# A two-block transformer on one core: the row factor of five RMS norms applied to the outputs of the linears that follow

## The reference, cut to what matters

```
def rmsnorm(x, g):
    y = xf * lax.rsqrt(jnp.mean(xf * xf, axis=-1, keepdims=True) + RMS_EPS)
    return (y * g).astype(x.dtype)

def hybrid_layer(...):
    h = rmsnorm(x, norm_mix)
    proj = h @ w_in                     # q_a, k_a, v_a, f_a, q_b, kv_b, g_b, gate_a, gate_b
    ...                                 # fox attention, compression, nsa attention with partial_rope
    mixed = jax.nn.sigmoid(gate_a) * y_a + jax.nn.sigmoid(gate_b) * y_b
    x = x + mixed @ w_out
    h = rmsnorm(x, norm_mlp)
    return x + jnp.square(jax.nn.relu(h @ w_up)) @ w_down
```

## Time and profile before

| | |
|---|---|
| median of three runs | 2520.76 us (2517.28 to 2521.58) |
| the profiled execution's own time | 2515.49 us |
| its span | 2513.7 us, 30926 instructions |
| PE busy | 2370.2 us, 94% of the span |
| DVE, POOL, ACT busy | 1485.4, 1512.8, 604.9 us |
| mean granted clock of PE, as a share of full speed | 0.972 |

### The profile page before, as it was taken

How to read it: one execution, slowest core, us unless ns; L and a number is a source line. 1 busy time by engine, 2 the same in 40 slices (tenths; PEclk the granted TensorE clock), 3 DMA queues, 4 the chain that set the end, 5 groups by cost and what they waited for, 6 DMA issues and landing times.

```text
span 2513.7 us, 30926 instructions
## 1 busy us (share of the span) xinstructions
PE 2370.2 (94%) x11516; PEld 1930.5 (77%) x11516; DVE 1485.4 (59%) x1955; ACT 604.9 (24%) x1305; POOL 1512.8 (60%) x677
## 2 busy tenths in 40 slices
PE   4987999999998999999999999989899999999998
PEld 4675778888876778888778888768688877788886
DVE  6798546675142156998485084340569985770742
ACT  3214612221012134342121021121253431210210
POOL 3670058888865641335778788655513348697884
PEclk9998989999999999999999999999999999999999
DMA  4220023223322310111323333223201113233322
GB/s 168 76 84 9 1 67 101 93 100 100 101 85 83 118 59 18 51 43 59 92 76 101 97 96 100 85 78 107 76 10 51 43 53 96 71 104 97 97 96 75
DMA packets 53694, 195.87 MB, mean 78 GB/s; under 512 B 5952, under 2 KB 5952, under 8 KB 53312
## 3 DMA queue, kind: packets, MB, share of 16 engines
q1 hardware_dynamic: 51408, 187.72, 23.6%
q10 hardware_dynamic: 2160, 6.37, 0.7%
HBM read 191.97 MB, written 2.10 MB: 77 GB/s over the span
## 4 chain that ended last, share of the span: by engine, by line
PE 68%; DVE 25%; issue 3%; ACT 1%; POOL 1%; DMA 0%; DVEq 0%; SPq 0%; POOLq 0%; ACTq 0%
PE bank L386 19%; PE bank L387 19%; PE bank L388 19%; DVE sg L1103 4%; PE bank L478 3%; DVE sg L1101 3%; PE bank L509 3%; DVE cols L1115 2%; DVE cols L1129 2%; DVE conv_acc L1044 2%; PE bank L489 1%; DVE on L1134 1%; DVE tmp L1396 1%; DVE cmp_g L1303 1%; PE bank L451 1%
## 5 line engine op out<-in xcount | busy, mean ns | idle before, releaser
L336 POOL TENSOR_TENSOR w_hi<-w_raw,zero 128x1024 fp32r<-128x1024 f32 x336 | 659.6, 1963 | 948.9 <-PE bank L388 923.5
L339 POOL TENSOR_TENSOR w_lo<-w_raw,w_hi 128x1024 fp32r<-128x1024 f32 x336 | 855.7, 2547 | 26.4
L386 PE MATMUL bank<-hn_hi,w_hi 128*128 128x512 f32 x1632 | 667.1, 409 | 20.8 <-DVE hn_lo L1027 14.3
L388 PE MATMUL bank<-hn_hi,w_lo 128*128 128x512 f32 x1632 | 643.0, 394 | 0.0
L387 PE MATMUL bank<-hn_lo,w_hi 128*128 128x512 f32 x1632 | 642.8, 394 | 0.0
L386 PEld LDWEIGHTS bank<-hn_hi,w_hi 128*128 128x128 f32 x1632 | 311.6, 191 | 91.7 <-issue 23.3
L388 PEld LDWEIGHTS bank<-hn_hi,w_lo 128*128 128x128 f32 x1632 | 310.5, 190 | 67.3
L387 PEld LDWEIGHTS bank<-hn_lo,w_hi 128*128 128x128 f32 x1632 | 311.5, 191 | 64.1 <-issue 4.9
L1152 DVE TENSOR_TENSOR x<-bank,x 128x512 f32<-128x512 f32 x64 | 44.3, 692 | 467.3 <-PE bank L388 467.3
L386 PE MATMUL bank<-hid_hi,w_hi 128*128 128x512 f32 x688 | 267.6, 389 | 0.0
L387 PE MATMUL bank<-hid_lo,w_hi 128*128 128x512 f32 x688 | 267.6, 389 | 0.0
(11 more groups left out here) (270 smaller groups left out, 3140.4 us busy)
## 6 DMA issues: line engine op xcount, KB each, us to landing
w_raw<-wstream SPq DMA_DIRECT2D x352, 512.0 KB, 3.6
x<-xT SPq DMA_DIRECT2D x4, 512.0 KB, 9.7
out<-yout ACTq DMA_DIRECT2D x8, 256.0 KB, 2.2
mem_x<-memT SPq DMA_DIRECT2D x1, 1024.0 KB, 15.9
lnc<-lncount ACTq DMA_DIRECT2D x1, 1024.0 KB, 4.8
cs<-trig ACTq DMA_DIRECT2D x2, 512.0 KB, 3.4
par<-params ACTq DMA_DIRECT2D x1, 707.5 KB, 6.4
fc<-fconst ACTq DMA_DIRECT2D x1, 592.0 KB, 8.7
```

Of the source, the lines that this page charges most:

```text
L336: nc.gpsimd.tensor_tensor(w_hi[:, slot, :], w_raw[:, slot, :], zeros, ALU.add).then_inc(w_rounded, 1)
L339: nc.gpsimd.tensor_tensor(w_lo[:, slot, :], w_raw[:, slot, :], w_hi[:, slot, :].bitcast(f32), ALU.subtract).then_inc(w_split, 1)
L386: nc.tensor.matmul(ps[bank][:, 0:cols_], wh, a_h, start=c == 0, stop=False)
L388: mm = nc.tensor.matmul(ps[bank][:, 0:cols_], wl, a_h, start=False, stop=c == chunks - 1)
```

## The change

**Norms 2 to 6.** ACT writes `hn_hi = x*g` straight from the residual, chunk by chunk as tiles are added (`norm_ahead`), and VectorE writes `hn_lo = x*g - hn_hi` inside `add_residual`. The row factor is kept in an SBUF tile `rs` (128 x 512) and multiplied into linears' outputs: by a VectorE multiplication in PSUM (`scale`), or within the instruction that takes the output out. PE starts the next pair of tiles on unscaled activations and has `norm_mean` after its chunk 3 and `norm_spread` behind it.

**Layers' inputs.** `HEAD2` is reordered (and the weight stream with it): the forget gate first, compression inputs third and fifth. VectorE multiplies the rotary table `cs2` by `rs` once a layer; the rotation reads the unscaled PSUM bank. VectorE's queue is in order, and its rotation of job i stands behind its `scale` of job i + 2.

**Gates.** VectorE takes gate tiles out (times `rs`), ACT applies Tanh of half the value in place, and `mix` uses 1 + tanh and a factor 0.5: no reciprocal is left.

**Feed-forward.** UP1 is pipelined by one step; in the layers relu and factor are one VectorE instruction, and ACT makes both the square (into `sq`) and its rounded copy.

```diff
-        HEAD2 = [("cmp", 0), ("cmp", 1), ("gate", 0)] + [("kz", i) for i in range(4)]
+        HEAD2 = [("gate", 0), ("kz", 0), ("cmp", 0), ("kz", 1), ("cmp", 1), ("kz", 2), ("kz", 3)]
...
-            def linear_pair(ta, tb, ready):
+            def linear_pair(ta, tb, ready, n=None):
                 for c in range(DC):
                     linear(ta, hn_hi, hn_lo, S, DC, ready, part=(c, c + 1))
                     linear(tb, hn_hi, hn_lo, S, DC, part=(c, c + 1))
+                    if n is not None and c == 3:
+                        norm_mean(n)
+                if n is not None:
+                    norm_spread(n)
...
-                        if kind == "gate":
-                            pe.wait_ge(*took(t))
-                            turn_tile(fgs[:, :], 4, TT, 32).then_inc(fg_turned, 1)
-                    if 0 <= i - 2 < len(jobs) and tiles[jobs[i - 2]][0] == "gate":
+                    if i == 2:
+                        pe.wait_ge(*took(jobs[0]))
+                        turn_tile(fgs[:, :], 4, TT, 32).then_inc(fg_turned, 1)
+                    if i == 4:
                         pe.wait_ge(fg_log, l + 1)
...
+            def norm_ahead(n, ts_):
+                for c in range(DC):
+                    act.wait_ge(dve_took, tiles[ts_[c]][6])
+                    A(hn_hi[:, c, :], x[:, c, :], ACT.Identity, scale=pcol(NORM_G[n], c)).then_inc(norm_hi, 1)
...
+                    A(sq[:, c % 2, :], x[:, c, :], ACT.Square).then_inc(norm_sq, 1)
+                act.wait_ge(norm_sum, n + 1)
+                A(rt[:, 0:TT], ps[7][:, 0:TT], ACT.Sqrt, bias=pcol("eps")).then_inc(norm_rt, 1)
+                act.wait_ge(norm_row, n + 1)
+                A(rs[:, :], ps[7][:, :], ACT.Copy).then_inc(rs_kept, 1)
...
-                        A(sg[:, g, :], ps[3][:, :], ACT.Exp, scale=-1.0).then_inc(act_took, 1)
+                        act.wait_ge(*took(gate_tiles[g]))
+                        A(sg[:, g, :], sg[:, g, :], ACT.Tanh, scale=0.5).then_inc(gated, 1)
...
+            def scale(t):
+                dve.wait_ge(blocks_done, filled(t))
+                bank = ps[tiles[t][4]]
+                V.tensor_tensor(bank[:, :], bank[:, :], rs[:, :], ALU.mult).then_inc(rs_applied, 1)
...
-                            link(V.tensor_scalar(sg[:, g, :], sg[:, g, :], 1.0, None, ALU.add))
-                        part = slice(quarter * P, (quarter + 1) * P)
-                        link(V.reciprocal(sg[:, g, part], sg[:, g, part]))
+                        dve.wait_ge(blocks_done, filled(gate_tiles[g]))
+                        V.tensor_tensor(sg[:, g, :], ps[3][:, :], rs[:, :], ALU.mult).then_inc(dve_took, 1)
...
                     V.tensor_tensor(x[:, m, :], ps[tiles[t][4]][:, :], x[:, m, :], ALU.add).then_inc(dve_took, 1)
-                    if n is not None and m >= 2:
+                    if n is not None and 2 <= m < DC - 1:
+                        norm_add(n, m - 1)
+                    if n is not None and n < 7:
+                        dve.wait_ge(norm_hi, DC * n + m + 1)
+                        V.scalar_tensor_tensor(out=hn_lo[:, m, :], in0=x[:, m, :], scalar=pcol(NORM_G[n], m),
+                                               in1=hn_hi[:, m, :].bitcast(f32), op0=ALU.mult,
+                                               op1=ALU.subtract).then_inc(norm_lo, 1)
+                    if n is not None and m == DC - 1:
                         norm_add(n, m - 1)
...
-                    if m == 1:
-                        link(V.tensor_scalar(sg[:, 15, :], sg[:, 15, :], 1.0, None, ALU.add))
-                        link(V.reciprocal(sg[:, 15, :], sg[:, 15, :]))
```

More of the change, by code:

```diff
@@ L258, in build, with idx_of_rope @@
             LIN.append(ph)
+        def idx_of_rope(t):
+            return tiles[t][1] + (4 if tiles[t][0] == "kr" else 0)
         def filled(t):
@@ L269, in build @@
         NORM_AFTER = {2: OUT1, 3: DN1, 4: LIN[0]["out"], 5: LIN[0]["down1"], 6: LIN[1]["out"], 7: LIN[1]["down1"]}
+        SCALED = {}
+        for t in UP1 + [t for ph in LIN for t in ph["in"] if tiles[t][0] in ("gate", "kz", "cmp", "v")]:
+            SCALED[t] = len(SCALED) + 1
         NORM_G = {0: "mix_g", 1: "mem_g", 2: "ffn_g", 3: "norm_mix0", 4: "norm_mlp0", 5: "norm_mix1",
@@ L651, in _ @@
                 linear(t, mix_hi, mix_lo, S, DC)
[L652 to L653 removed]
+            linear_pair(UP1[0], UP1[1], (norm_lo, 2 * DC), 2)
             for t in UP1[2:]:
@@ L918, in _ @@
                 ph = LIN[l]
-                norm(3 + 2 * l, x, hn_hi)
-                act.wait_ge(blocks_done, B_L + l * LAYER_BLOCKS)
+                norm_ahead(3 + 2 * l, LIN[0]["down1"] if l else DN1)
                 act.dma_start(cs2[:, :, :], trig2).then_inc(trig2_loaded, 16)
@@ L974, in _ @@
                     act.wait_ge(mix_full, DC * l + m + 1)
-                    A(mx_hi[:, m, :], tmp[:, m % 3, :], ACT.Copy).then_inc(mix_rounded, 1)
-                norm(4 + 2 * l, x, hn_hi)
+                    A(mx_hi[:, m, :], tmp[:, m % 3, :], ACT.Copy, scale=0.5).then_inc(mix_rounded, 1)
+                norm_ahead(4 + 2 * l, ph["out"])
                 for half in range(2):
@@ new lines, in _ @@
+                    if j < 22:
+                        scale(UP1[2 * j + k])
+                    p_ = j - 1
+                    if p_ >= 0 and k == 0:
+                        dve.wait_ge(*took(UP1[2 * p_ + 1]))
+                        dve.wait_ge(ff_silu, p_ + 1)
+                        V.tensor_tensor(tmp[:, p_ % 3, :], yrow[:, (2 * p_) % 4, :], yrow[:, (2 * p_ + 1) % 4, :],
+                                        ALU.mult).then_inc(ff_full, 1)
+                    if p_ >= 0 and k == 1:
+                        dve.wait_ge(ff_full, p_ + 1)
+                        dve.wait_ge(ff_hi, p_ + 1)
+                        V.tensor_tensor(hid1_lo[:, p_, :], tmp[:, p_ % 3, :], hid1_hi[:, p_, :].bitcast(f32),
+                                        ALU.subtract).then_inc(ff_lo, 1)
@@ new lines, in _ @@
+                    if j < 22:
+                        t = UP1[2 * j + k]
+                        ch, y, src = j + 22 * k, yrow[:, (2 * j + k) % 4, :], ps[tiles[t][4]]
+                        dve.wait_ge(ff_lin, 2 * j + k + 1)
+                        link(V.scalar_tensor_tensor(out=y[:, 1:S], in0=src[:, 0:S - 1], scalar=pcol("ffn_w", 3 * ch),
+                                                    in1=y[:, 1:S], op0=ALU.mult, op1=ALU.add))
+                        V.scalar_tensor_tensor(out=y[:, 0:S - 1], in0=src[:, 1:S], scalar=pcol("ffn_w", 3 * ch + 2),
+                                               in1=y[:, 0:S - 1], op0=ALU.mult, op1=ALU.add).then_inc(dve_took, 1)
@@ L1280, in _ @@
                 ph = LIN[l]
-                norm(3 + 2 * l, x, hn_hi, hn_lo)
                 dve.wait_ge(blocks_done, B_L + l * LAYER_BLOCKS)
@@ L1304, in _ @@
                         ins.then_inc(cmp_full, 1)
-                    if 0 <= i - 1 < len(jobs) and tiles[jobs[i - 1]][0] == "gate":
+                    if i == 3:
                         dve.wait_ge(fg_turned, l + 1)
@@ L1330, in _ @@
                                                op1=ALU.add).then_inc(fg_log, 1)
-                    if 0 <= i - 2 < len(jobs) and tiles[jobs[i - 2]][0] == "gate":
+                    if i == 5:
                         dve.wait_ge(fg_cum, l + 1)
@@ L1440, in _stream @@
         kv = kv_b.reshape(D, 6, P)
-        out += [_blocks(a) for a in (kv[:, 0], kv[:, 1], fg, k_a)]
+        k_a = [k_a[:, c * P:(c + 1) * P] for c in range(4)]
+        out += [_blocks(a) for a in (fg, k_a[0], kv[:, 0], k_a[1], kv[:, 1], k_a[2], k_a[3])]
         w1 = [_blocks(a) for a in i["cmp_w1_2"][l]]
```

199 lines of the change are left out of this document (110 added, 89 removed).

## The result

| | before | after |
|---|---|---|
| median of 4 runs, us | 2520.46 | 2472.95 |
| lowest to highest | 2517.28 to 2521.58 | 2472.80 to 2476.49 |
| span of the profiled execution | 2513.7 | 2471.1 |

The ratio is 0.9816, 95% interval 0.9801 to 0.9832: faster by 47.5 us by the medians, by 42.6 us by the two profiled executions. The forecast was 39.4 us less and a median of 2481 (2468 to 2499).

What follows compares the result with a forecast made beforehand. PE, busy 94% of the span, was taken to bound the kernel. Terms 43.4 + 4.2 + 2.2 - 1.4 - 8.4 - 0.6 = 39.4 us off the median 2520.8 gave 2481; range 2468 to 2499.

Steps and rivals of the forecast that it cites:

- The norms, 43.4: Norms 2 to 6: loss falls from 60.9 us to 3.5 a norm, as the pair's matmuls cover VectorE's chain; gain 43.4 us.
- PEclk full there: Sign expected in the changed profile: PE's granted clock full at norms 2 to 6, with waits for `acc` under 0.5 us.
- rival of a slow TensorE: Around the norms' mean: PE's clock halves or the sum comes late, 2 to 2.5 us more a norm; 2493; chance 0.14.
- Mix tail, 4.2: Behind `mix`: without the last gate's reciprocal PE waits 0.7 instead of 2.0 us twice, one half clock goes; gain 4.2 us.
- Last kr rotation, -8.4: Layers' inputs: rotation behind a scaling makes PE wait 3.8 us, 3.2 more, plus 1.0 for lower clock, twice; -8.4 us.
- qb +2.2: Layers' inputs: the `qr` rotation wait of twice 1.1 us goes away, since the additions read PSUM; +2.2 us.
- last v -0.6: Layers' inputs: the last `v` tile goes over VectorE to ACT; 0.3 us lost, twice.
- The wait for the logarithm, 7.1 left: Layers' inputs: PE's wait for the forget gate's logarithm stays at 7.1 us; bounds 5 and 9.
- The gate's turn, -1.4: Layers' inputs: PE wants the forget gate's tile after job 2 and waits 0.7 us, twice; -1.4 us.
- nsa attention, 0: Nsa attention: VectorE's handover of bank 3 and the dropped reciprocals are both hidden under PE; 0 us.
- slower rival: Nsa attention: VectorE's in-order handover of bank 3 delays PE 32 times; at 2 us each 64 us, 2545; chance 0.06.
- VectorE bounds UP1: Feed-forward UP1: a two-tile step takes 12.3 instead of 10.9 us if nothing is absorbed; 2504; chance 0.07.

Runs made afterwards that it cites:

- mean_first: The changed kernel with the norm's mean and spread done ahead of the pair of linears at norms 2 to 6; 2533.5 us, ratio to before 1.0055.
- mean_early: The changed kernel with the norm's mean behind chunk 2 of the pair instead of chunk 3; 2494.0 us, ratio to before 0.9882.
- gates_only: The kernel before with the gates part of the change alone (Tanh instead of Exp and reciprocal); 2525.0 us, ratio to before 1.0012.
- rope_first: The changed kernel with the rotation of job i - 2 ahead of the scaling of job i in VectorE's queue; 2464.6 us, ratio to before 0.9776.
- cum_later: The changed kernel with the forget gate's turn, cumulative sum and VectorE's taking of it each one job later; 2462.4 us, ratio to before 0.9781.
- old_gates: The changed kernel with gates in the old manner (Exp, plus 1, reciprocal), scaled in place in bank 3; 2503.5 us, ratio to before 0.9923.
- calm_after: The changed kernel with GpSimd's split of the fourth weight block waiting for VectorE's memory-norm sum of squares; 2477.3 us, ratio to before 0.9834.

## Why the prediction was right, and where it was off

*The norms, 43.4.* Right in mechanism and nearly in size. The windows give 60.9 - 16.2 = 44.7, in which the wait at the gate's turn already counts as a loss. I had the last addition end 5.4 to 5.8 us behind the residual matmul and it ended at 5.3 (352.64 to 357.96). mean_first shows that without the order of the pair nothing is left of this term. The sign "PEclk full there" failed at norm 3 (0.93): eight matmuls of about 0.63 us behind the mean, some 1.6 us, a piece of the rival of a slow TensorE. VectorE's chain and the cover came out equal within 0.2 us, and mean_early shows what six matmuls less would have cost; that they met so closely was partly luck.

*Mix tail, 4.2.* 0.6 instead of 0.7 us of waiting; the half clock in layer 0 is gone. By the `out` linears' length (47.2 and 45.6 us before, 44.2 twice after) it was 4.4. gates_only, where PE waits 0.6 us behind `mix` too, shows that it is the gates' part. The Tanh needed no further table load: both traces have 20, and none stands in nsa attention, where 16 Tanh a layer alternate with Exp.

*Last kr rotation, -8.4; qb +2.2; last v -0.6.* Forecast 3.8 us of waiting, measured 3.50, by just the chain that was added up:
```profile
874.42 0.70 DVE L1049 TENSOR_TENSOR bank<-bank,rs 128x512 f32<-128x512 f32 x1 [15.57 <-PE bank L399]
875.03 0.68 DVE L1409 SCALAR_TENSOR_TENSOR t<-bank,cs 128x512 f32<-128x512 f32 x1
875.63 0.69 DVE L1411 TENSOR_TENSOR bank<-bank,cs 128x512 f32<-128x512 f32 x1
876.35 0.68 DVE L1416 TENSOR_TENSOR ksw<-bank,t 64x512 f32<-64x512 f32 x1
877.05 0.69 DVE L1417 TENSOR_TENSOR ksw<-bank,t 64x512 f32<-64x512 f32 x1
877.89 2.05 PE L468 MATMUL bank<-tmp,fc 128*128 128x512 f32 x2 [3.50 <-DVE ksw L1417]
878.95 1.42 PE L397 MATMUL bank<-hn_hi,w_hi 128*128 128x512 f32 x1
880.16 0.63 PE L398 MATMUL bank<-hn_lo,w_hi 128*128 128x512 f32 x1
```
The stage grew by 3.8 and 3.6 us, forecast (8.4 - 2.2 + 0.6) / 2 = 3.4. The handing of `v` over VectorE to ACT was put too low: PE's wait for it went from 1.7 to 3.1 us in all. The half clock behind the gap costs more than the 1.0 put down for it: the rotation's two matmuls take 2.05 instead of 1.10, and eight of 0.63 follow. rope_first settles the cause: with the scaling out of the way, wait and half clock go.

*The wait for the logarithm, 7.1 left.* This step failed in size: 4.6 remained, twice 2.5 us more of gain, just outside the bounds of 5 and 9. I had let the chain in VectorE's queue end as late after job 4 as before. What stands ahead of it in the queue is a compression of two instructions with both inputs in SBUF, here before, after and in mean_first (layer 0):
```profile
758.61 5.36 DVE L1303 TENSOR_TENSOR cmp_g<-cmp_t,par 128x496 f32<-128x496 f32 x2 [2.54 <-ACT cmp_t L953]
...
740.01 3.54 DVE L1365 TENSOR_TENSOR cmp_g<-cmp_t,par 128x496 f32<-128x496 f32 x2 [3.09 <-ACT cmp_t L981]
...
767.13 5.15 DVE L1363 TENSOR_TENSOR cmp_g<-cmp_t,par 128x496 f32<-128x496 f32 x2 [2.48 <-ACT cmp_t L979]
```
mean_first has the changed kernel's order of jobs, and its wait is 5.9: there the compression took 1.6 us longer than in the changed kernel, and the wait is 1.3 longer. So about half of the 2.5 us comes with the new place of the gate and a chain that is 0.5 us shorter, and the other half with where these two instructions fell among GpSimd's splits, which stood still for 0.84 us at 741.8 in the changed kernel. The prediction had no term for that half; it was luck. cum_later took nearly all of the wait that was left.

*The gate's turn, -1.4.* 0.70 us in layer 0 as forecast, none in layer 1; it lies within norm 3's window and so within the 44.7.

*nsa attention, 0.* 11.51 instead of 11.42 us for four units: -2.9. This term was put at nothing because the work hides under PE, and VectorE is indeed idle for 5.3 of 11.51 us; but PE was waiting for bank 3 already, and the instruction that empties it became 0.09 us longer (rows under gates_only). The handover of bank 3, of which the slower rival spoke, is real, but 0.09 us a time and not 1.2; old_gates shows what 0.6 more would cost.

*UP1 and the rest of the feed-forward, 0.* From the first matmul of norm 2's pair to that of norm 3's it is 362.0 us, norm 2's mean and spread included, so the sign against the prediction (over 362 for UP1 with DN1) did not come. The rival that VectorE bounds UP1 falls.

*The sum and the median.* As measured the terms are 44.7 + 4.4 + 5.0 (logarithm) - 7.4 (rotations and inputs) - 2.9 = 43.8, beside 42.6 between the two profiled executions and 39.4 forecast; the miss of the logarithm and that of nsa attention partly cancel. The forecast then took the sum from the median of before, and the medians differ by 47.5: the measured 2473 lies 8 us under the 2481. Of these, 3 are in the terms. The other 5 are the distance between before's profiled execution and its median, which the changed kernel, profiled at its median, does not have. That the runs of before often had a longer start than the 292.5 us of the profiled one would explain it, but no profile of them exists, and it stays open.

## What to carry to other kernels

A factor that can be applied behind a linear was worth nothing here by itself. What paid is the work that may then stand ahead of the factor, and its length has to be measured to the matmul: here 24 of them cover a chain of 5.3 us but for 0.1, and 18 don't, for about 13 us in five norms. What tells is the start of the matmul that waits: when it comes 0.05 us behind the end of what it needs at every norm, it is waiting, though PE's list of waits shows nothing.

After a move, read every queue in which the moved instruction now has something ahead of it that waits for the very engine one wants to free. Two such places (a scaling ahead of a rotation, a sum asked for one job too soon) held 28 us here, and both were cured by exchanging lines.

## What the runs showed of the hardware

VectorE's 128 x 256 subtraction with both inputs in SBUF takes 0.41 us while GpSimd stands still and 1.7 to 2.2 beside its splits, while an instruction of the same tile with one input in PSUM keeps its 0.47 in between (rows of calm_after above). The Trainium skill (SBUF — State Buffer, Who interferes with whom) says that a VectorE instruction with two SBUF inputs and a GpSimd instruction that reads SBUF exclude each other, and the trace agrees. What I had not expected is how this acts on the time: in these profiles GpSimd's split waits for TensorE to free a slot of weights, so whether it meets these short instructions depends on TensorE. In rope_first PE came to full clock 2.5 us sooner than in the changed kernel (38.0 instead of 40.5 us), and its start was the longer one by 8 us: the splits began at 47.2 instead of 48.1 and met all five additions, 9.5 us instead of 4.1. These are 5.4 of the 8 us; the rest was not followed.

TensorE's granted clock did not fall for the mean's 16 matmuls of one column: at norm 2, with a gap of 0.1 us, the window above has 1.00. It did fall at norm 3, where a gap of 0.2 us stood ahead of them (0.93), and in mean_early behind 1.3 us. Whether it is the gap or something else that differs at norm 3 stays open. That the kernel before spreads over 2514 to 2526 us in the 37 runs beside the experiments is more than the 8 us of the start, and the rest of it was not explained.
